# A long convolution in a two-block transformer: tables loaded one stage earlier, stacked filter rows, a shared short convolution

## What is computed

```python
u = short_conv(a @ w_in, conv_w)              # (256, 3072), three taps per channel
v, x1, x2 = split(u)
z_pos = [t, cos(f w), -sin(f w)]              # (256, 33)
hdn = sin(freq * (z_pos @ w1 + b1)); hdn = sin(freq * (hdn @ w2 + b2)); hdn = sin(freq * (hdn @ w3 + b3))   # (256, 64)
filt = (hdn @ filt_out).reshape(256, 2, 2, 1024) * window      # forward and backward filter of two orders
z = v
for n, gate in enumerate((x1, x2)):
    z = gate * (irfft(rfft(z, 512) * rfft(k_n)) + z * skip[n]) # k_n: forward filter, 0, flipped backward filter[1:]
out = z @ w_out
```

## Time and profile before

| | us |
|---|---|
| median of 3 runs | 2266.15 (2261.7 to 2268.45) |
| the profiled execution, its own time | 2265.96 |
| its span in the trace | 2264.2 |
| long-convolution stage | 1838.2 to 2032.8 |

### The profile page before, as it was taken

How to read it: one execution, slowest core, us unless ns; L and a number is a source line. 1 busy time by engine, 2 the same in 40 slices (tenths; PEclk the granted TensorE clock), 3 DMA queues, 4 the chain that set the end, 5 groups by cost and what they waited for, 6 DMA issues and landing times. The chain is left out here.

```text
span 2264.2 us, 37426 instructions
## 1 busy us (share of the span) xinstructions
PE 2162.5 (96%) x15928; PEld 1922.4 (85%) x15928; DVE 1578.0 (70%) x2335; ACT 916.0 (40%) x1284; POOL 2.3 (0%) x8
## 2 busy tenths in 40 slices
PE   6999999999999999999999898999899999999998
PEld 5999999877899899968998687888699986758997
DVE  4877877646887788757877456376677777856545
ACT  3444443317544454335434453343454443115342
POOL 0000000000000000000000000000000000000000
PEclk7999999999999999999999899999999998999999
DMA  9866687430688688715986111300278741305551
GB/s 394 326 247 240 246 316 312 167 111 34 239 336 322 244 340 329 298 75 211 353 315 260 64 56 45 105 22 3 79 283 320 292 159 66 149 0 186 195 186 37
DMA packets 65748, 450.81 MB, mean 199 GB/s; under 512 B 8023, under 2 KB 9240, under 8 KB 12696
## 3 DMA queue, kind: packets, MB, share of 16 engines
q1 hardware_dynamic: 65624, 449.09, 51.6%
HBM read 448.01 MB, written 1.05 MB: 198 GB/s over the span
## 5 line engine op out<-in xcount | busy, mean ns | idle before, releaser
L512 PEld LDWEIGHTS banks<-ffn_h_split,ffn_weights_split 128*128 128x128 f32 x7392 | 898.7, 192 | 13.0 <-DVE ffn_weights_split L587 4.7
L512 PE MATMUL banks<-ffn_h_split,ffn_weights_split 128*128 128x256 f32 x7392 | 903.1, 284 | 6.3 <-DVE ffn_h_split L608 6.3
L750 DVE TENSOR_TENSOR ffn_weights_split<-weight_ring,ffn_weights_split 128x2048 fp32r<-128x2048 f32 x224 | 512.5, 2288 | 236.3 <-ACT ffn_weights_split L654 236.3
L654 ACT CAST ffn_weights_split<-weight_ring 128x2048 fp32r<-128x2048 f32 x224 | 426.0, 1902 | 174.7 <-PE banks L527 164.7
L527 PE MATMUL banks<-ffn_weights_split,ffn_hidden_split 128*128 128x512 f32 x1512 | 355.0, 390 | 1.8 <-DVE ffn_hidden_split L687 1.8
L527 PEld LDWEIGHTS banks<-ffn_weights_split,ffn_hidden_split 128*128 128x128 f32 x1512 | 279.8, 188 | 57.6 <-DVE ffn_hidden_split L687 2.2
L622 ACT ACTIVATE ffn_arena<-banks 128x256 f32<-128x256 f32 x154 | 59.0, 383 | 501.4 <-PE banks L512 501.4
L710 DVE CUSTOM_DVE_ANT_0 weight_ring<-weight_ring,first_arena,cols 128x1024 f32<-128x1024 f32 x200 | 245.4, 1280 | 0.4 <-ACT first_arena L664 0.4
L694 DVE TENSOR_TENSOR ffn_arena<-banks,ffn_arena 128x256 f32<-128x256 f32 x154 | 64.8, 421 | 46.6 <-ACT ffn_arena L622 46.5
L1388 PE MATMUL banks<-h,weight_ring 128*128 128x256 f32 x384 | 88.1, 389 | 0.0
L1388 PEld LDWEIGHTS banks<-h,weight_ring 128*128 128x128 f32 x384 | 74.1, 195 | 12.7 <-issue 2.5
(11 more groups left out here) (366 smaller groups left out, 2270.5 us busy)
## 6 DMA issues: line engine op xcount, KB each, us to landing
weight_ring<-in_weights SPq DMA_DIRECT2D x407, 1024.0 KB, 4.9
first_arena<-in_norm_rows SPq DMA_DIRECT2D x12, 512.0 KB, 7.2
first_arena<-in_c_rows SPq DMA_DIRECT2D x4, 512.0 KB, 11.1
first_arena<-in_ctx_rows SPq DMA_DIRECT2D x2, 1024.0 KB
h<-in_ctx SPq DMA_DIRECT2D x1, 1024.0 KB, 18.0
side<-in_x SPq DMA_DIRECT2D x1, 1024.0 KB
x<-in_x_rows SPq DMA_DIRECT2D x1, 1024.0 KB
hyena_arena<-in_hy_filt SPq DMA_DIRECT2D x1, 1024.0 KB
```

The source lines that it names most:

```text
L512: last = nc.tensor.matmul(bank[:, half * T:half * T + T], w[:, x, sl], hs[:, k, y, :], start=(k == 0 and x + y == 0), stop=(k == DT - 1 an ...
L654: nc.scalar.copy(wsplit[:, c % S, 0, :], raw).then_inc(self.split_hi.sem, 1)
L750: nc.vector.tensor_tensor(wsplit[:, c % S, 1, :], core.wbuf[:, (self.first + at(c)) % NSLOT, :], wsplit[:, c % S, 0, :].bitcast(F32), ALU. ...
```

## The change

Four edits:
- The eight tables get an SBUF tensor of their own that exists from the feed-forward on. Their DMAs leave the long-convolution stage and are issued by SP in the feed-forward, between the load of chunk slot 31 and that of slot 32. TensorE gets ten 128 x 128 matmuls ahead of `project(0)`.
- The middle tap of the short convolution is computed by ScalarE from PSUM, behind the copy (two activations with a per-channel scale). VectorE has two operations left for each group.
- On VectorE the low part of chunk c + 2 is made behind `conv(c)`, not ahead of it.
- The third hidden layer gives its 64 rows twice. ScalarE makes `plus` (both halves sin) and `minus` (first half negated), with the first column of the second half zeroed; `hy_filt` holds forward filter rows above backward filter rows. One matmul with 128-row operands gives the sum, one the difference, and `window` is two products.

```diff
@@ FeedForward.sp
         self.tail.sp_rows(sp)
+        for dst, src in self.ahead:
+            sp.dma_start(dst, src).then_inc(self.core.counter("inputs_loaded_ahead").sem, 16)
         core.load_range(sp, max(self.first + NSLOT, self.first + at(20)), self.first + self.slots.total() + NSLOT)
@@ hyena, sync
-            for dst, src in loads:
-                sp.dma_start(dst, src).then_inc(tables.sem, 16)
             core.load_ahead(sp)
@@ hyena, tensor
+            for _ in range(10):
+                nc.tensor.matmul(core.ps[7][:, 0:P], core.ident[:, :], core.ident[:, :], start=True, stop=True)
...
-                nc.tensor.matmul(core.ps[2][0:64, 0:T], lhs[:, :], rhs[:, :], start=True, stop=True).then_inc(mlp_ready.sem, 1)
+                rows = P if i == 2 else 64
+                nc.tensor.matmul(core.ps[2][0:rows, 0:T], lhs[:, :], rhs[:, :], start=True, stop=True).then_inc(mlp_ready.sem, 1)
...
-                    pe.wait_ge(sine.sem, sine.base + 3)
-                for dr in range(2):
-                    at = (dr * 2 + n) * D + half * 512
-                    last = nc.tensor.matmul(core.ps[pair_of(m) + dr][:, :], hid[:, t * P:t * P + P], b["hy_filt"][:, at:at + 512],
+                    pe.wait_ge(sine.sem, sine.base + 4)
+                at = n * D + half * 512
+                for e, both in enumerate((plus, minus)):
+                    last = nc.tensor.matmul(core.ps[pair_of(m) + e][:, :], both[:, t * P:t * P + P], b["hy_filt"][:, at:at + 512],
                                             start=True, stop=True)
@@ hyena, scalar
-                nc.scalar.copy(raw[:, slot:slot + 2, 1:T + 1], core.ps[c % 2][:, :].rearrange("p (a t) -> p a t", a=2))\
-                    .then_inc(raw_copied.sem, 1)
+                nc.scalar.copy(raw[:, slot:slot + 2, 1:T + 1], core.ps[c % 2][:, :].rearrange("p (a t) -> p a t", a=2))
+                for e in range(2):
+                    i = 2 * c + e
+                    last = nc.scalar.activation(z[:, i, :] if i < DT else u[:, i - DT, :], core.ps[c % 2][:, e * T:e * T + T],
+                                                ACT.Identity, bias=0.0, scale=core.col("hy_conv")[:, 24 + i:25 + i])
+                last.then_inc(raw_copied.sem, 1)
...
+                nc.scalar.activation(plus[:, :], t1[:, :], ACT.Sin).then_inc(sine.sem, 1)
+                act.wait_ge(sine.sem, sine.base + 3)
+                nc.scalar.activation(minus[0:64, :], plus[0:64, :], ACT.Identity, bias=0.0, scale=-1.0)
+                nc.scalar.copy(minus[64:P, 1:T], plus[64:P, 1:T])
+                nc.scalar.activation(minus[64:P, 0:1], t1[64:P, 0:1], ACT.Identity, bias=0.0, scale=0.0)
+                nc.scalar.activation(plus[64:P, 0:1], t1[64:P, 0:1], ACT.Identity, bias=0.0, scale=0.0).then_inc(sine.sem, 1)
@@ hyena, vector
             def conv(c):
-                if c + 2 < 12:
-                    core.low(dve, nc.vector, first + 2 * (c + 2), w_lo)
                 dve.wait_ge(raw_copied.sem, raw_copied.base + c + 1)
...
-                    conv_step(nc.vector.tensor_scalar(y, x[:, 0:T], w[:, i:i + 1], None, ALU.mult))
-                    conv_step(nc.vector.scalar_tensor_tensor(y, x[:, 1:T + 1], w[:, 24 + i:25 + i], y, ALU.mult, ALU.add))
+                    conv_step(nc.vector.scalar_tensor_tensor(y, x[:, 0:T], w[:, i:i + 1], y, ALU.mult, ALU.add))
                     last = nc.vector.scalar_tensor_tensor(y, x[:, 2:T + 2], w[:, 48 + i:49 + i], y, ALU.mult, ALU.add)
                 last.then_inc(conv_done.sem, 1)
+                if c + 2 < 12:
+                    core.low(dve, nc.vector, first + 2 * (c + 2), w_lo)
...
-                f_step(nc.vector.tensor_tensor(kp[:, t, sl], core.ps[bank][:, :], b["hy_win"][:, t, sl], ALU.mult))
-                f_step(nc.vector.tensor_tensor(bw[:, :], core.ps[bank + 1][:, :], b["hy_win"][:, t, sl], ALU.mult))
-                if t == 0:
-                    f_step(nc.vector.memset(bw[0:1, :], 0.0))
-                f_step(nc.vector.tensor_tensor(km[:, t, sl], bw[:, :], kp[:, t, sl], ALU.subtract))
-                nc.vector.tensor_tensor(kp[:, t, sl], kp[:, t, sl], bw[:, :], ALU.add).then_inc(windowed.sem, 1)
-                dve.wait_ge(windowed.sem, windowed.base + 4 * n + m + 1)
+                nc.vector.tensor_tensor(kp[:, t, sl], core.ps[bank][:, :], b["hy_win"][:, t, sl], ALU.mult)
+                nc.vector.tensor_tensor(km[:, t, sl], core.ps[bank + 1][:, :], b["hy_win"][:, t, sl], ALU.mult)\
+                    .then_inc(windowed.sem, 1)
```

More of the change, by code:

```diff
@@ L2427, in hyena @@
     fwd, inv, hid, t1, t2 = b["hy_fwd"], b["hy_inv"], b["hidden"], b["t1"], b["t2"]
-    tables = take("inputs_loaded_ahead", 16 * len(loads))
-    loaded = tables.base + 16 * len(loads)
+    plus, minus = b["plus"], b["minus"]
+    tables = take("inputs_loaded_ahead", 16 * 8)
+    loaded = tables.base + 16 * 8
     raw_copied, padded, conv_done = take("hy_raw_copied", 12), take("hy_padded", 1), take("conv_done", 12)
-    mlp_ready, mlp_steps, sine = take("hy_mlp_ready", 3), take("dve_steps", 18), take("hy_mlp_sine_done", 3)
-    f_ready, windowed, f_steps = take("hy_filter_ready", 8), take("hy_windowed", 8), take("hy_filter_steps", 28)
+    mlp_ready, mlp_steps, sine = take("hy_mlp_ready", 3), take("dve_steps", 18), take("hy_mlp_sine_done", 4)
+    f_ready, windowed = take("hy_filter_ready", 8), take("hy_windowed", 8)
     r_ready, r_copied = take("hy_ring_ready", 24), take("hy_ring_copied", 24)
@@ L2435, in hyena @@
     y_ready, gated, g_steps = take("hy_y_ready", 8), take("hy_gated", 16), take("hy_gate_steps", 16)
-    conv_steps = take("conv_steps", 48)
+    conv_steps = take("conv_steps", 24)
     h_hi, h_lo, w_lo, hs = take("ffn_h_hi", DT), take("ffn_h_lo", DT), take("linear_weights_lo", 12), b["hs"]
@@ L2637, in _ @@
         def _(dve):
-            conv_step, f_step, p_step, g_step = (Steps(dve, m) for m in (conv_steps, f_steps, p_steps, g_steps))
+            conv_step, p_step, g_step = (Steps(dve, m) for m in (conv_steps, p_steps, g_steps))
             mlp_step = Steps(dve, mlp_steps)
@@ L3032, in program @@
                 recurrent_mixer(y)
-            with phase("ffn_3", 8192, True):
-                f, spread, mix = ffn_space()
-                crow, xn = {(1, 0): carve(D)}, carve(TT, D)
-                tail = Tail(core, "rms", x, vec(2, 2), 1.0, tail_space(spread, mix, None, xn),
-                            modulation=(vec(2, 4), vec(2, 3)), affine=norm("norm2", 2), out=hf, spread=0, signals=2)
-                project = Linear(core, y, f, tail)
-                tail = Tail(core, "rms", x, vec(2, 5), 1.0, tail_space(spread, mix, None, xn),
-                            modulation=(vec(3, 1), vec(3, 0)), affine=norm("norm1", 3), out=hf, spread=1)
-                ffn_a = FeedForward(core, hf, f, tail, sides_of(5, crow), before=project,
-                                    vector=(crow[(1, 0)], broadcast(2, "c_rows")), split_next=True)
-                run(core, project, ffn_a)
-            with phase("hyena", 29504, False), nc.sbuf_tensor("hyena_h_split", [P, DT, 2, T], F32R) as hyena_hs:
-                hyena_mixer(y, hyena_hs)
+            with nc.sbuf_tensor("hyena_tables", [P, 6656], F32) as hyena_tables:
+                tables = carve_tables(hyena_tables)
+                with phase("ffn_3", 8192, True):
+                    f, spread, mix = ffn_space()
+                    crow, xn = {(1, 0): carve(D)}, carve(TT, D)
+                    tail = Tail(core, "rms", x, vec(2, 2), 1.0, tail_space(spread, mix, None, xn),
+                                modulation=(vec(2, 4), vec(2, 3)), affine=norm("norm2", 2), out=hf, spread=0, signals=2)
+                    project = Linear(core, y, f, tail)
+                    tail = Tail(core, "rms", x, vec(2, 5), 1.0, tail_space(spread, mix, None, xn),
+                                modulation=(vec(3, 1), vec(3, 0)), affine=norm("norm1", 3), out=hf, spread=1)
+                    ffn_a = FeedForward(core, hf, f, tail, sides_of(5, crow), before=project,
+                                        vector=(crow[(1, 0)], broadcast(2, "c_rows")), split_next=True,
+                                        ahead=[(v, a[n]) for n, v in tables.items()])
+                    run(core, project, ffn_a)
+                with phase("hyena", 23360, False), nc.sbuf_tensor("hyena_h_split", [P, DT, 2, T], F32R) as hyena_hs:
+                    hyena_mixer(y, hyena_hs, tables)
             with phase("ffn_4", 8192, True):
```

44 lines of the change are left out of this document (24 added, 20 removed).

## The result

The changed kernel takes 2251.62 us (median of 4, 2249.8 to 2252.25), the kernel before beside it 2267.30 (median of 4, 2261.7 to 2269.82): ratio 0.9933, 95% interval 0.9913 to 0.9953. Timed once more on another chip it took 2253.80 (5 runs) against 2263.31 (11 runs), ratio 0.9952 [0.9939, 0.9965].

The account below looks back on a forecast made before the run. TensorE, busy 96% of the span, was taken as the bound, with VectorE's chain setting the filters' start. Gains of 6.5 us through project(6) and 3.7 at the first inverse gave 2266.15 - 10.2 = 2256.0 us, range 2250.5 to 2262.0.

Parts of the forecast that it names:

- Start of the stage: Ten warm-up matmuls ahead of project(0): project(0) ends 0.5 us later, at 1847.2 instead of 1846.67.
- Filters earlier: Before the filters: earlier weight and shorter VectorE chain, less added ScalarE work, start them at 1876.7 instead of 1880.90, 4.2 us.
- Clock behind the filters: Filters to project(6): low clock costs 2.6 us (bounds 0 and 4.9) instead of 4.9, since operands now have 128 rows.
- Matmuls of 64 and 128 rows: Filter matmuls with stacked rows: they keep their number and columns; no full-clock gain was counted.
- First inverse: At the first inverse: the 2.0 us window wait and 1.7 us of slow inverse behind it go, together 3.7 us.
- Feed-forward, middle, and the rest at 0: Tables in the feed-forward cost 0, covered by the weight lead; product, spectrum and inverse to the end are untouched.
- first rival: Low clock persists behind the filters or warm-up costs its full price: 2.3 or 1 us, together 3.3, 2259.3 us; chance 0.19.
- table load follows the sine: ScalarE rival: Identity with a scale after Sin forces table switches, 2.6 to 4 us, 2259.5 us; chance 0.06.
- third rival: Tables delay feed-forward weights: at 82 GB/s TensorE stands 23 us, +13, 2279 us; nothing below 14; chance 0.05.
- fourth rival: VectorE's chain shortens but another link is late; only the 3.7 us at the inverse stays, 2262.5 us; chance 0.07.
- Better than forecast: Clock never falls at the filters or the stage's start: 13 us gained, 2253 us; chance 0.08.

Follow-up runs that it names:

- after_again: The changed kernel itself, unaltered, profiled and timed once more on another chip: 2253.80 us, ratio 0.9952.
- u_warm: The changed kernel without its ten idle matmuls ahead of project(0): 2252.56 us.
- u_tables: The changed kernel with the eight tables issued at the start of the long-convolution stage again, ahead of its weights: 2254.79 us.
- hold: The changed kernel with three and six idle products added around the last transposes before the filters, where TensorE waits: 2251.16 us.
- rows64: The changed kernel with filter matmuls cut to the first 64 of 128 operand rows, same count and columns: 2253.29 us.
- win4: The changed kernel with four VectorE operations per window again, plus the memset, over the 128-row matmuls: 2256.34 us.
- more2: The changed kernel with the 1 MB window table loaded twice more behind the tables in the feed-forward: 2251.35 us.
- u_taps: The changed kernel with the middle taps on VectorE again and ScalarE only copying: 2253.74 us.
- tuned: The changed kernel with four idle products behind the barrier, seven ahead, first plus operands signalled early, low part 5 after phase(2): 2248.60 us.
- best: The changed kernel without barrier idle products, with three and six before the filters, first plus operands signalled early, low part 5 after phase(2): 2247.47 us.

## Why the prediction held, point by point

The shares of the 13.5 us, by the steps of the forecast of 10.2:

- **Start of the stage.** Forecast 0.5 us lost; hidden(0) came 0.27 later in this profile and 1.86 later in after_again. For the chain the end of project(0) counts, and the weight was issued 11.1 us behind zero, where 11.8 was forecast. u_warm shows no gain from the warm-up.
- **Filters earlier.** Forecast 4.2, measured 45.47 - 40.10 = 5.4. The chain of VectorE was 19.47 us (19.4 forecast), and ScalarE's part from the end of that chain to the filters 1.52 (0.47 + 1.3 forecast). The rest of the difference is the chain's start, 19.1 us behind zero instead of 20.1: the weight was issued 0.7 sooner, was there the forecast 4.9 after, and rounding, copy and tap pair took 3.1 instead of 3.4. But the forecast credited the whole of these 4.9 instead of ten to the moved tables, and u_tables gives them 1.4 of 5.2. The rest came with the tables' layout or order, which the forecast had only as an argument against a rival. The taps' price of 0.47 for one sat right: 477 ns mean over 24. The Trainium skill ("ScalarE: Activation LUTs", section "What ACT_TABLE_LOAD costs") gives 186 ns plus 0.833 ns an element plus 93 ns for each pointer operand, an estimate of 492 ns here; the trace is 3% below it.
- **Clock behind the filters.** Forecast 20.9 us for two pairs and two projects, measured 19.78. The loss to the low clock was 1.70 (against hold), not 2.6. The reason given, that 128-row operands bring the clock back sooner, is what rows64 shows: 3.65 us. It was taken between its bounds of 0 and 4.9 without a row that could decide, so a miss of 0.9 is no merit. Three misses of about the same size, all the same way, make the 3.3 us by which the stage did better than forecast: 1.2 in the filters' start, 0.9 here, 1.2 in the next term.
- **Matmuls of 64 and 128 rows.** I had written that the filter matmuls keep their number and columns, and counted no gain at full clock. They gained 0.3 with the first two pairs (18.34 against 18.08 in hold) and 0.9 with the last two. That step was wrong by about 1.2 us, and the trace of before could have told: its spectra (L2540), eight passes of 512 columns with 128 rows like the new filters, went from 1917.89 to the next row at 1920.93 in 3.04 us, the 64-row filters (L2499) at the same clock in 3.62 (1894.99 to 1898.61).
- **First inverse.** Forecast 2.0 + 1.7; measured 2.04 and 1.70, and win4 gives both back.
- **Feed-forward, middle, and the rest at 0.** All held. With 2.1 MB more it is still 0.

The rivals: the low clock did not persist, and against before hidden(0) came only 0.27 us later in the first profile. In six of ten profiles it came 1.3 to 1.9 later, which is the full price that the first rival named; that half of it came true without deciding. No table load follows the sine: ScalarE has one, for the first of them, and Identity runs at 416 ns right behind Sin. The tables held up nothing in the feed-forward. The third rival began at 14 us for the tables; more2's 5.3 MB would be 12.6 us at 424 GB/s, still below it, so that point was not reached. The fourth rival's "another link is late" is refuted by u_tables and u_taps: both are worth 2.3 to 2.7 us each, so the chain was read rightly. "Better than forecast" was priced at 13 us for a clock that never falls; the stage came to 13.5 with the clock still falling, since the other two terms were too small.

Three things stay open. Whether the tables' layout or their order made the weight 3.8 us less late was not tried. Why the clock falls during the idle products at the barrier in one execution and not in another isn't told by any run here. Nor is it why zero itself lies up to 6 us apart between executions, though in all profiles it was so before the tables were issued.

## What to carry to other kernels

When an engine's chain feeds one wait of TensorE, cost the chain from the event that starts it: here a late weight, full VectorE and the clock behind the gap were three prices of one wait, and each part of the edit paid into it. Matmuls that use half the rows aren't cheaper in time, and after a gap they are dearer, since the clock stayed low for as long as they ran and some 3 us more; where the sum of two half-row products is wanted, stack them. Put idle products where TensorE waits in any case and the clock is seen to fall, and measure them: ahead of the work, behind the barrier, they were delay in every profile here. And when a weight queues behind other loads, look at the layout and the order of those loads before moving them: here the two together were worth 3.8 us of the weight's delay and the move 1.4.

## What the runs showed of the hardware

- After waits of 0.72 and 1.85 us with 1.06 us of transposes between them TensorE's grant fell to 0.50 (1.2 GHz) as the filters began; with 0.75 and 0.38 us (tuned) it stayed at 1.00. With 128-row matmuls it was full again within 5 us, with 64-row ones at equal count and columns after 10 us, although TensorE was busy without a pause in both (rows64 against the changed kernel).
- After the same 2.87 us gap at the barrier the grant was 0.50 in the profile of before and stayed at full in u_warm and best (1.00 in 1835 to 1841 and in 1836 to 1844).
- A pair of filter groups of eight 512-column passes took 3.03 us start to start with 128 rows and 3.62 with 64, at full clock.
- A weight behind the same amount of other loads was rounded 10.1 us after its issue (before) and 6.3 (u_tables); with nothing queued ahead, 4.7 to 5.0.
- One execution's profile says little about the time of another: the same program ahead of the stage took up to 6 us more or less (zero at 1831.96 to 1837.97), more than any single part of this change was worth.
